# First-layer projections by seven half-size products, in the projection stage and behind the attention

## What is computed

```
proj = jnp.einsum('bsd,df->bsf', h, w_in).astype(jnp.float32)
qa, ka, va, qb, kb, vb, lr_f, lr_b, gate = _split(
    proj, (A_WIDTH, A_WIDTH, A_WIDTH, B_K_WIDTH, B_K_WIDTH, B_V_WIDTH, B_GATE_RANK, B_GATE_RANK, MIX_WIDTH))
oa = dilated_attention(heads(qa, A_HEADS), heads(ka, A_HEADS), heads(va, A_HEADS), rel_bias)
g_f = jax.nn.log_sigmoid(lr_f @ up[0] + gb_[0]) / B_GATE_NORMALIZER
...
ob = bidirectional_gated_scan(qh, kh, heads(g_f, B_HEADS), kh, heads(g_b, B_HEADS), heads(vb, B_HEADS))
y = jnp.concatenate([oa, ob], axis=-1) * jax.nn.silu(gate)
return jnp.einsum('bsf,fd->bsd', y.astype(h.dtype), w_out)
```

## Time and profile before

| | |
|---|---|
| time, median of three runs | 4108.58 us |
| time of the profiled execution | 4102.72 us |
| its span | 4101.0 us |
| TensorE busy (matmul) | 3579.0 us, 87% of the span |
| VectorE busy | 1812.7 us, 44% |
| ScalarE busy | 1081.5 us, 26% |
| GpSimd busy | 1183.6 us, 29% |
| mean granted clock of TensorE | 0.924 of full speed |
| prologue | 0 to 25.6 us |
| projection stage, first to last product | 25.6 to 193.9 us |
| attention: lead | 207.2 to 251.2 us |
| attention: slots 0 to 95 | 261.3 to 684.8 us |
| first instruction of the next stage | 691.0 us |

### The profile page before, as it was taken

How to read it: one execution, slowest core, us unless ns; L and a number is a source line. 1 busy time by engine, 2 the same in 40 slices (tenths; PEclk the granted TensorE clock), 3 DMA queues, 4 the chain that set the end, 5 groups by cost and what they waited for, 6 DMA issues and landing times. The chain is left out here.

```text
span 4101.0 us, 47003 instructions
## 1 busy us (share of the span) xinstructions
PE 3579.0 (87%) x16369; PEld 2330.3 (57%) x16369; DVE 1812.7 (44%) x4038; ACT 1081.5 (26%) x2206; POOL 1183.6 (29%) x948
## 2 busy tenths in 40 slices
PE   8889998888798999999989598998966776949996
PEld 4645676667443676576647346665556775424442
DVE  0025552333374266566576352233478577241001
ACT  1023333333242233333342351221203212111111
POOL 0000000333243355555555353001303445211110
PEclk9999998899899999999999797998987888969998
DMA  3264532121532111211211633113234722346996
GB/s 115 72 176 147 160 118 85 61 97 57 195 147 86 53 56 50 60 55 50 59 51 36 240 140 81 45 43 117 90 101 128 254 91 75 144 181 232 318 322 230
DMA packets 409824, 494.01 MB, mean 120 GB/s; under 512 B 70514, under 2 KB 314506, under 8 KB 409603
## 3 DMA queue, kind: packets, MB, share of 16 engines
q1 hardware_dynamic: 380983, 457.42, 33.6%
q0 software_dynamic: 4608, 16.78, 1.6%
q10 hardware_dynamic: 24012, 16.97, 1.3%
HBM read 362.32 MB, written 128.77 MB: 120 GB/s over the span
## 5 line engine op out<-in xcount | busy, mean ns | idle before, releaser
L821 POOL TENSOR_TENSOR hgrn_queries<-hgrn_qd,hgrn_pair_decay 128x640 f32<-128x640 f32 x192 | 279.6, 1476 | 291.4 <-PE hgrn_ps_a L936 256.5
L395 PE MATMUL gla_bg_ps<-gla_bg_w,xT 128*128 128x256 f32 x768 | 199.8, 408 | 4.0 <-DMA gla_bg_w<-in_w_in_ab_dram 4.0
L871 PE MATMUL hgrn_ps_w<-xT,hgrn_ring 128*128 128x512 f32 x432 | 195.7, 599 | 1.8 <-PEq L34 1.8
L395 PEld LDWEIGHTS gla_bg_ps<-gla_bg_w,xT 128*128 128x128 f32 x768 | 154.3, 206 | 38.8 <-issue 11.0
L1473 PE MATMUL end_ps_z<-end_w,end_yT 128*128 128x512 f32 x384 | 168.7, 599 | 1.6 <-DMA end_w<-in_w_out_ab_dram 1.0
L2560 PE MATMUL end_ps_z<-end_w,end_yT 128*128 128x512 f32 x384 | 168.4, 598 | 0.8 <-ACT end_yT L2488 0.8
L391 PE MATMUL att_bg_ps<-xT,att_bg_w 128*128 128x512 f32 (+1 forms) x288 | 137.6, 618 | 13.3 <-POOL att_ident L1780 13.3
L45 POOL MEMSET gla_ident<- 128x128 f32 x1 | 0.2, 204 | 483.9 <-POOLq L34 483.9
L871 PEld LDWEIGHTS hgrn_ps_w<-xT,hgrn_ring 128*128 128x128 f32 x432 | 81.5, 193 | 94.3 <-issue 94.0
L871 PE MATMUL hgrn_ps_w<-hgrn_xs,hgrn_wsum 128*128 128x512 f32 x288 | 129.8, 598 | 5.3 <-ACT hgrn_sig L1153 5.3
L1041 DVE TENSOR_TENSOR hgrn_k_end<-hgrn_kd,hgrn_end_decay 128x128 f32<-128x128 f32 x168 | 127.3, 797 | 9.2 <-issue 2.6
(11 more groups left out here) (645 smaller groups left out, 7700.9 us busy)
## 6 DMA issues: line engine op xcount, KB each, us to landing
expw_wg<-in_exp_w_gate_dram SPq DMA_DIRECT2D x16, 2048.0 KB, 10.3
expw_wu<-in_exp_w_up_dram SPq DMA_DIRECT2D x16, 2048.0 KB, 16.3
expw_wd<-in_exp_w_down_dram SPq DMA_DIRECT2D x16, 2048.0 KB, 21.9
att_w_ada<-in_ada_w_dram SPq DMA_DIRECT2D x24, 1024.0 KB, 6.4
hgrn_ring<-in_w_in_c_dram SPq DMA_DIRECT2D x18, 1024.0 KB, 5.4
end_gt<-gate_l SPq DMA_DIRECT2D x16, 768.0 KB, 8.5
hgrn_ring<-in_w_in_c_dram SPq DMA_DIRECT2D x24, 512.0 KB, 5.5
hgrn_o<-hgrn_o_stage SPq DMA_DIRECT2D x192, 64.0 KB, 1.6
```

What stands on the lines that cost most here:

```text
L395: last = pe.matmul(bank[0:job.rows, q * job.width:(q + 1) * job.width], job.acts[:, k, t * P:t * P + job.rows], w[:, k, 0:job.width], star ...
L821: pool.tensor_tensor(queries[:, d, s, :].rearrange("p (b a c) -> p b a c", b=POINTS, a=PC), q, f, ALU.mult).then_inc(queries_done, 1)
L871: last = pe.matmul(bank[:, :], a[:, k, :], x(k), start=(fresh and k == 0), stop=(k == HK - 1), skip_group_check=True)
```

## The change

Every unit of 256 output columns becomes a problem of two by two blocks: two halves of the 1024 channels, two halves of the tokens, two halves of the columns. In place of eight half-size products there are seven (called SNAP1, PLAIN, SNAP21, SNAP22, JOIN22, JOIN21 and LAST in the code), on sums of blocks. The sums of `xT` (three buffers `xs`, and one half of `xT` changed in place) are made by VectorE at the start of the projection stage and kept for the attention. The first op of the scan stage undoes the one in place. Four sums of the weights of each unit are made by GpSimd (`sums`). Of the seven results ScalarE moves four from PSUM to a stage, and VectorE adds three onto a stage (`join`, a read of PSUM plus a read of the stage).

A CHANNEL unit is then 28 products of 128x512 in place of 32, and a TOKEN unit 112 products of 128x128 in place of 64 of 128x256, since a product now moves half of the 256 columns.

The narrow gate input goes from the attention's lead to the head of the projection stage; its weights are loaded in the prologue. One ring of three units holds the weights in both stages, and the projection stage loads the first two units of the attention. The modulation is cut to 48 units of 128 columns (16 with two rows, 32 with one), 6 products in a slot, so that its ring takes half the room; a unit's sum on TensorE is due one slot after its last product in place of two, and its accumulator has three buffers.

```
-def dilated_attention(nc, tag, qT, kT, vpad, vectors, attn, jobs, sT, ada_w, ada):
+def dilated_attention(nc, tag, qT, kT, vpad, vectors, attn, xT, xs, ring, wsum, bg_stage, units, sT, ada_w, ada):
...
-    ADA_W = 256
+    ADA_W = 128
+    PER = 6
...
-        bg = Background(sb, sem, pbank, jobs, HEADS * ST, 3, 3, 3, lead=LEAD)
+        bg = Halves(sem, xT, xs, ring, wsum, bg_stage, [pbank(f"bg_ps{b}") for b in range(3)], units, HEADS * ST, 2, lead=LEAD)
...
-            return unit_ends[u] // 3 + 2
+            return unit_ends[u] // PER + 1
...
-            bg.begin(sp)
             sp.wait_ge(consts, 1)
             load(0)
+            bg.load(sp, 2)
             load(1)
             load_ada(0)
...
-                if g + 1 in unit_due and unit_due[g + 1] + 3 < ADA_UNITS:
-                    load_ada(unit_due[g + 1] + 3)
+                if g in unit_due and unit_due[g] + 3 < ADA_UNITS:
+                    load_ada(unit_due[g] + 3)
...
-                    wait(dve, summed, u - 1)
+                    wait(dve, summed, u - 2)
...
             dve.wait_ge(consts, 1)
+            for g in range(LEAD):
+                bg.join(dve, g)
             for g in range(HEADS * ST):
...
                 if g > 1:
                     move_out(g - 2)
+                bg.join(dve, LEAD + g)
+            bg.join(dve, LEAD + HEADS * ST)
```

More of the change, by code:

```diff
@@ L49, in make_identity, with prologue @@
     pool.drain()
-def prologue(nc, tag, src, dst, rel_bias, buckets, vectors, vpad, c, c_ctx, sT, weights, wbuf):
+def prologue(nc, tag, src, dst, rel_bias, buckets, vectors, vpad, c, c_ctx, sT, weights, ring, low_w, low_at):
     T = SEQ // P
-    W = wbuf[0].shape[2]
     with ExitStack() as ctx:
@@ L1642, in dilated_attention @@
         w_ada = sb("w_ada", [P, 3, KB, ADA_W])
-        acc, ones, row = sb("acc", [P, 2, 2, ADA_W]), sb("ones", [P, 1]), sb("row", [1, 2, 2, ADA_W])
+        acc, ones, row = sb("acc", [P, 3, 2, ADA_W]), sb("ones", [P, 1]), sb("row", [1, 2, 2, ADA_W])
         ps_a = pbank("ps_a")
@@ L1780, in _ @@
             pool.memset(ident[0:1, 0:1], 1.0).then_inc(consts, 1)
+            for u in range(len(units)):
+                bg.sums(pool, u)
         @block.tensor
@@ L1823, in total @@
                 wait(pe, row_moved, u)
-                pe.matmul(ps_a[0:1, 0:n * ADA_W], ones[:, :], acc[:, u % 2, 0:n, :], start=True, stop=True).then_inc(summed, 1)
+                pe.matmul(ps_a[0:1, 0:n * ADA_W], ones[:, :], acc[:, u % 3, 0:n, :], start=True, stop=True).then_inc(summed, 1)
             pe.wait_ge(consts, 1)
@@ L1934, with low_rank_scan @@
 RANK = 16
-def low_rank_scan(nc, tag, heads, V, qT, kT, vals, lowT, up, gate_bias, out, g_scale, q_scale, jobs):
+def low_rank_scan(nc, tag, heads, V, qT, kT, vals, lowT, up, gate_bias, out, g_scale, q_scale, xT, jobs):
     PC = P // CH
@@ L2257, in prepare @@
                     grown(h, p - 5)
+            low_rows = slice(0, KB // 2)
+            dve.tensor_tensor(xT[:, low_rows, BANK:SEQ], xT[:, low_rows, BANK:SEQ], xT[:, low_rows, 0:BANK], ALU.add).then_inc(restored, 1)
             dve.wait_ge(consts, 1)
@@ L4814, in network @@
             w = w_in_ab[0]
-            with ExitStack() as first_weights:
-                wbuf = [first_weights.enter_context(nc.sbuf_tensor(f"in0_wbuf{b}", [P, KB, 256], F32)) for b in range(2)]
-                prologue(nc, "pro", x[0], xT, rel_bias, buckets, vectors, vpad, c_2, c_ctx_2, sT, w, wbuf)
-                project(nc, "in0", [
-                    Job(CHANNEL, xT, SEQ, w, 0, 256, 2, qa),
-                    Job(CHANNEL, xT, SEQ, w, A, 256, 2, ka),
-                    Job(TOKEN, xT, SEQ, w, 2 * A, 256, 2, vpad[VPAD:VPAD + SEQ, :]),
-                ], loaded=wbuf)
@@ L4823, in network @@
[L4823 to L4830 removed]
+            low_at = 5 * A + B
@@ new lines, in network @@
+            channels = lambda col, dst: [Unit(CHANNEL, w, col + UNIT_W * n, dst, UNIT_W * n) for n in range(A // UNIT_W)]
+            tokens = lambda col, dst, width: [Unit(TOKEN, w, col + UNIT_W * n, dst, UNIT_W * n) for n in range(width // UNIT_W)]
+            first = channels(0, qa) + channels(A, ka) + tokens(2 * A, vpad[VPAD:VPAD + SEQ, :], A)
+            second = channels(3 * A, qb) + channels(4 * A, kb) + tokens(5 * A, vb, B)
+            with ExitStack() as shared:
+                held = lambda n, *shape: shared.enter_context(nc.sbuf_tensor(n, [P, *shape], F32))
+                ring, wsum = held("l0_ring", 3, KB, UNIT_W), held("l0_wsum", 3, KB // 2, P)
+                stage, xs = held("l0_stage", 4, BANK), held("l0_xs", 3, KB // 2, BANK)
+                with nc.sbuf_tensor("l0_low_w", [P, KB, 2 * RANK], F32) as low_w:
+                    prologue(nc, "pro", x[0], xT, rel_bias, buckets, vectors, vpad, c_2, c_ctx_2, sT, w, ring, low_w, low_at)
+                    project_halves(nc, "in0", xT, xs, ring, wsum, stage, first, second[0:2], low_w, low)
+                dilated_attention(nc, "att", qa, ka, vpad, vectors, attn, xT, xs, ring, wsum, stage, second, sT, ada_w_2[0], ada)
```

196 lines of the change are left out of this document (183 added, 13 removed).

## The result

The changed kernel takes 4127.85 us (median of 5, 4121.16 to 4134.27) against 4108.64 before (median of 5 taken with it): ratio 1.0051, 95% interval 1.0033 to 1.0068. It is slower, where no change was forecast. The profiled execution took 4121.16 us against 4102.72, so 18.4 us are to be found between the two traces.

A forecast was written before the change was run, and what follows sets the result against it. TensorE was taken as the bound, busy 421 of 422 us in the attention's slots. The terms summed to -0.7 us against the profiled 4102.7 (4102; 4107.9 from the median), so 4105 was forecast, range 4077 to 4132.

The forecast's parts named there:

- Projection stage and prologue: Before the attention: fewer and narrower products less the added narrow input, -5.7 us; one more DMA in the prologue, +1.
- Start of the attention: Shorter lead, but the first score waits for modulation weights queued on SyncE behind two pairs of heads: -8.8 us.
- Products in the slots: Attention slots: 8 channel products fewer, 6.9 us, and 4 cheaper token units, 11.3 us: -18.2 us.
- Joins: Attention slots: 21 joins ahead of a bias on VectorE delay the score, up to 1.35 us each: +15 us.
- Fourth pair: Near slot 53: twenty head loads on SyncE delay a modulation load and row store; stall 7.5 plus 1.5 clock: +9 us.
- Ring loads: Single-row slots: in two iterations a modulation load stands behind a ring load waiting for a fill: +4 us.
- GpSimd: Attention slots: weight sums delay VectorE's modulation products by 18 us, of which VectorE's slack takes most: +3 us.
- the second rival: VectorE becomes the bound in single-row slots 43 to 85, narrow ones above all: +26, 4131 us; chance 0.20.
- Scan stage: Its first op, restoring `xT`, is hidden in VectorE's wait: 0 to +2 us if it slows GpSimd's constants.
- The clock behind the waits: Half clock after TensorE idles: about 1.5 us behind the fourth pair's stall; at the attention's start, equal to before.
- the two rivals with a real chance: In the attention: waits are covered, 4082 us, chance 0.30; VectorE becomes the bound, 4131 us, chance 0.20.
- The third: Rival on 128-column records: weight loads exposed, 107 ns on each of 1344 records, +144, 4249 us; chance 0.02.

The follow-up runs named there:

- the second run: The changed kernel with the attention's first three modulation loads issued ahead of the ring load and the second pair of heads: 4108.69 us, ratio 1.0009 to the kernel before.

## Why the prediction was wrong

The sum came to -0.7; the same terms by the trace:

- Projection stage and prologue, forecast -4.7: the stage gave 6.0 (forecast 5.7) and the prologue cost 0.5 (forecast 1), both right. The attention starts 7.75 us earlier, since 2.3 more came from the shorter gap ahead of it, of which nothing was said: luck.
- Start of the attention, forecast -8.8: -9.1. Right, by the wait that was named; the second run shows that the order on SyncE sets it.
- Products in the slots, forecast -18.2: -14, and 2.5 back for the totals, which had no term. The prediction named both ends, 0.111 and 0.1175 us a record, and took the one from a run of 12; the slots' short runs have 0.120.
- Joins, forecast +15: 13.1 in 16 waits. The mechanism and its size were right; 6.8 us of clock behind them were missing.
- Fourth pair, forecast +9: 7.7 and 2.0 of clock. The place and the twenty loads were right. The sum priced the path through VectorE; the wait ended with the row store, which the prediction named beside it, and either path gives 7.7. The load took 9.3 us to land, where 7 was taken for its half size; half the bytes did not shorten it here.
- Ring loads, forecast +4: one wait of 3.2 us, wholly hidden behind GpSimd's.
- **GpSimd, forecast +3: 9.5 us alone, 12.8 with the place it shares.** This step failed: the 18 us of delay were worked out nearly right (448 products at a mean of 399 against a median of 351 ns: 21.5), but "VectorE's slack takes most" was an average. The four sums come within 5.8 us, in one slot or two, and a slot's slack, 4.2 less 3.6 by the prediction's own numbers, is 0.6 us. It is the place and part of the price of the second rival; the condition it named (a mean product above 0.45 us) never came about. By the Trainium skill ("SBUF — State Buffer", Who interferes with whom) an op is locked out while the other engine holds the ports; the trace agrees, with 1461 ns for a product of 351.
- Scan stage, forecast 0 to +2: +1.5, by what was named, GpSimd's constants slowed beside the restoring op.
- **The clock behind the waits, forecast 1.5 us at one place: 20.** This is the larger failure. Each wait was priced as its length. The prediction counted half clock at the start, where TensorE had idled for long, and behind the fourth pair, and took a wait of 1.4 us to cost 1.4. The run with waits added to the kernel before shows that such waits bring the half clock, in a kernel without joins or weight sums.

By these terms the sum is some +24 in place of -0.7: 18 of the difference is clock and 6 GpSimd with the ring loads; the products and totals add 6.5, and the luck at the start, the smaller joins and a small rest take back 6. With the scan's 1.5 and the -7.6 of scatter in the later stages it comes to 18, of the 18.4 between the two traces. The range, to 4132, held the time; the forecast within 4092 to 4118 did not.

Of the two rivals with a real chance, the waits were not covered, and VectorE was not the bound: with the joins one step later and the sums gated it carried the same work, and TensorE waited 2 us. The third fell with the 0.112 us of the long runs of 128-column records.

What stays open is why one wait of 1.4 us is followed by half clock and the next is not; the same wait of the same kernel was in one execution and was not in another.

## What to carry to other kernels

Price a new wait of TensorE at its length and, where the clock is full all around it, at some more for the clock: behind 16 waits of 1.2 to 2.1 us 13.7 us were lost (0.9 each on average), behind nine of the changed kernel 15.4 (1.7 each), and behind the one of 6.9 us 2.0. So many short waits cost more than one long one of the same sum. Count half clock only where the engine works. Ask of each op added to the engine that feeds TensorE not how much it takes but what stands behind it: the same join ahead of the bias or behind it was 21 us. Slack counts slot by slot, so spread what comes in bursts (GpSimd's sums, twenty loads in a row), and where two causes meet at one wait, taking one away shows nothing.

## What was not expected of the hardware

- Waits of TensorE of 1.2 to 2.1 us in an otherwise unbroken stream were followed, 0.4 to 2.6 us after their end, by stretches of some 3.4 us or 6.8 us at 1.2 GHz while TensorE was busy (7 of 16 in one kernel; 7 of 9 in another, and 7 of 9 again when that one was run once more, not the same seven).
- A VectorE op on 128x2 that reads one SBUF tile took 1.27 us in place of 0.17 beside a GpSimd sum of 1.27 us. So not only ops with two SBUF inputs are held. The Trainium skill ("SBUF — State Buffer", Who interferes with whom) counts ops in a two-port mode of VectorE among those that take the lock; no row here shows an op's mode.
- It goes the other way too: a GpSimd op on 128x128 took 2.08 us in place of 0.29 beside a VectorE add of 2.29 us with two SBUF inputs, and TensorE, which waited for it, started 1.5 us later.
- A modulation load of half the size took 9.3 us to land behind the fourth pair, where the full size had taken 8.5.
